# Gate rows of a hybrid mixer layer: a stage of their own, or computed beside the mLSTM projection

## The reference, cut to what matters

```python
h = _rms(x, p['norm1_g']) * (1 + sc1) + sh1
(mq, mk, mv, mi, mf, mo, gqkv, ga, gb, gz, aq, ak, av, gates) = _split(h @ p['w_in'], IN_SPLITS)
# mLSTM gates, 4 heads, 2 directions
log_i = mi.reshape(B, T, 2, M_HEADS).astype(F32) + ig_b.astype(F32)
log_f = jax.nn.log_sigmoid(mf.reshape(B, T, 2, M_HEADS).astype(F32) + fg_b.astype(F32))
# delta rule gates
g = -jnp.exp(A_log.astype(F32)) * jax.nn.softplus(ga.reshape(B, T, 2, G_HEADS).astype(F32) + dt_bias.astype(F32))
beta = jax.nn.sigmoid(gb.reshape(B, T, 2, G_HEADS).astype(F32))
```

## Time and profile before

| | us |
|---|---|
| median of three timed runs | 6535.48 |
| profiled execution, its own time | 6504.0 |
| span of the profiled execution, first to last instruction | 6502.2 |
| first norm of layer 1, 99 to 130 us, PE busy | 9.84 of 31.00 |
| gate rows of layer 1, 130 to 176.5 us, PE busy | 24.32 of 46.50 |
| projection of the mLSTM, 189 to 305 us, PE busy | 115.96 of 116.00 |

### The profile page before, as it was taken

How to read it: one execution, slowest core, us unless ns; L and a number is a source line. 1 busy time by engine, 2 the same in 40 slices (tenths; PEclk the granted TensorE clock), 3 DMA queues, 4 the chain that set the end, 5 groups by cost and what they waited for, 6 DMA issues and landing times. The chain is left out here.

```text
span 6502.2 us, 69823 instructions
## 1 busy us (share of the span) xinstructions
PE 5261.9 (81%) x25140; PEld 3598.9 (55%) x25140; DVE 3462.5 (53%) x7471; ACT 1476.1 (23%) x3146; POOL 3234.1 (50%) x3088
## 2 busy tenths in 40 slices
PE   5878877995888888888768788679958888888877
PEld 4866767894444444443248768679944444444432
DVE  6154534226666666666361644341266666666663
ACT  4222123111222222222142221231112222222221
POOL 1222321124777777777612223211247777777775
PEclk8978988997999999999979889889979999999999
DMA  5110000216999999999852100102179999999998
GB/s 200 56 45 7 1 14 26 91 59 231 409 406 405 404 402 405 405 405 396 345 184 59 41 7 1 34 11 88 59 254 409 406 405 405 403 404 404 405 389 346
DMA packets 521162, 1531.89 MB, mean 236 GB/s; under 512 B 56478, under 2 KB 154718, under 8 KB 520552
## 3 DMA queue, kind: packets, MB, share of 16 engines
q0 software_dynamic: 369024, 1342.47, 52.5%
q1 hardware_dynamic: 149708, 184.85, 8.7%
q10 hardware_dynamic: 2080, 0.01, 0.0%
HBM read 1522.06 MB, written 5.09 MB: 235 GB/s over the span
## 5 line engine op out<-in xcount | busy, mean ns | idle before, releaser
L1897 PE MATMUL pb<-vb,x_diags 128*128 128x512 f32 x5120 | 2495.9, 611 | 611.9 <-DMA vb<-in_p_v,x_idx 597.2
L1758 DVE CUSTOM_DVE_ANT_0 ub<-ub,h 128x1024 f32<-128x1024 f32 x1280 | 1567.4, 1225 | 1061.3 <-DMA ub<-in_p_u,x_idx 1051.2
L1897 PEld LDWEIGHTS pb<-vb,x_diags 128*128 128x128 f32 x5120 | 873.1, 189 | 1513.3 <-issue 1268.5
L1697 POOL DMA_INDIRECT ub<-in_p_u,x_idx x1280 | 1293.7, 1011 | 500.9 <-issue 363.5
L1697 POOL DMA_INDIRECT vb<-in_p_v,x_idx x1280 | 1274.5, 996 | 410.7 <-issue 227.3
L1867 PEld LDWEIGHTS pb<-h2T,Wq 128*128 128x128 f32 x2560 | 459.2, 192 | 506.1 <-issue 503.7
L1837 ACT ACTIVATE x_diags<-identity,x_coefs 128x128 f32<-128x128 f32 x1280 | 416.6, 392 | 581.0 <-PE pb L1897 531.2
L1867 PE MATMUL pb<-h2T,Wq 128*128 128x128 f32 x2560 | 470.2, 275 | 1.6 <-DVE kT L1784 1.6
L250 PE MATMUL pb<-e_Whi,hS_hi 128*128 128x256 f32 x1280 | 381.6, 298 | 27.9 <-DVE e_Wlo L1595 27.8
L251 PE MATMUL pb<-e_Wlo,hS_hi 128*128 128x256 f32 x1280 | 359.5, 281 | 0.0
L252 PE MATMUL pb<-e_Whi,hS_lo 128*128 128x256 f32 x1280 | 359.0, 280 | 0.0
(11 more groups left out here) (383 smaller groups left out, 8453.6 us busy)
## 6 DMA issues: line engine op xcount, KB each, us to landing
adaW<-in_ada_w SPq DMA_DIRECT2D x24, 2048.0 KB, 9.4
e_Wg<-in_w_in SPq DMA_DIRECT2D x24, 1024.0 KB, 6.0
ub<-in_p_u,x_idx POOLq DMA_INDIRECT x1280, 6.9
vb<-in_p_v,x_idx POOLq DMA_INDIRECT x1280, 6.9
m_W<-in_w_in SPq DMA_DIRECT2D x16, 1024.0 KB, 5.6
Wq<-in_p_wq SPq DMA_DIRECT2D x8, 2048.0 KB, 16.0
g_W<-in_w_in SPq DMA_DIRECT2D x12, 1024.0 KB, 5.4
modAB<-mod_rows SPq DMA_DIRECT2D x16, 512.0 KB, 6.0
```

What stands on the lines that cost most here:

```text
L1697: G.indirect_dma_start(ring[:, n % RING, :], None, table, bass.IndirectOffsetOnAxis(ap=idx[:, i % LIVE, s:s + 1], axis=0)).then_inc(in_[n ...
L1758: V.tensor_tensor_reduce(out=ub[:, n % RING, :], in0=ub[:, n % RING, :], in1=h2[:, t, :], scale=1.0, scalar=0.0, op0=ALU.mult, op1=ALU.add ...
L1897: last = mm(pb[2 * (t % 2) + j][:, :], diag[:, n % DRING, :], vb[:, n % RING, 512 * j:512 * j + 512], start=(h == 0 and s == 0), stop=(h = ...
```

## The change

`stage_rows` is gone. `gate_rows` holds the same computation as pieces that `project` calls at certain places of its programs. The first norm no longer writes exact rows: ACT writes both halves of a tile's rounded rows from PSUM, DVE both halves of the low part, from PSUM and the rounded rows. The gate weights are split in two parts on POOL and multiplied by `product`, in the form of jobs 0 to 15. The projection uses banks 0 to 3, the gate products banks 4 to 7. The raw weight buffers go from three to two. Seven rows of a common buffer replace ten; its first four are later overwritten by the output gate. The scan of b no longer reads rows that reset it, but starts anew in each 128 tokens.

```diff
-                with ExitStack() as exact:
-                    hT = sb(exact, "hT", [P, KD, TOK])
-                    with stage():
...
-                        stage_norm(0, ahead=load_constants)
-                    with stage():
-                        stage_rows(l)
+                    stage_norm(0, ahead=load_constants, split=hS)
...
+                            if split:
+                                for j in range(2):
+                                    act.wait_ge(s_tr, 2 * t + j + 1)
+                                    S.activation(split[0][:, 4 * j:4 * j + 4, t * P:(t + 1) * P], v4(pb[2 * (t % 2) + j][:, :]), ACT.Copy).then_inc(s_evA, 1)
...
+                            if t >= 1 and split:
+                                for j in range(2):
+                                    dve.wait_ge(s_evA, 2 * t - 1 + j)
+                                    part = (slice(None), slice(4 * j, 4 * j + 4), slice((t - 1) * P, t * P))
+                                    V.tensor_tensor(split[1][part], v4(pb[2 * ((t - 1) % 2) + j][:, :]), split[0][part], ALU.subtract).then_inc(s_evV, 1)
...
+        def gate_rows(l, scope, rowbuf):
...
+            Z, e_, LF, LI, SG, m_, b = [rowbuf[:, j, :] for j in range(7)]
+            AI, WK, EM = Z, e_, LF
...
+            def gpsimd_after(pool, n):
+                if n != 0:
+                    return
...
+                link(G.tensor_copy(w16s[0][:, :, :, :], w16[:, :, :, :]))
+                link(G.tensor_tensor(w16s[1][:, :, :, :], w16[:, :, :, :], w16s[0][:, :, :, :], ALU.subtract))
...
+            def tensor_at(pe, i):
+                if i == 4:
+                    pe.wait_ge(r_wc, 16)
+                    for j, (w, done) in enumerate(((w1, r_p1), (w2, r_p2))):
+                        for k2, (o, n) in enumerate(HALVES):
+                            product(pb[4 + 2 * j + k2][:, 0:n], lambda a, k: w[a][:, k, :], lambda a, k: hS[a][:, k, o:o + n], KD).then_inc(done, 1)
+                elif i == 16:
+                    pe.wait_ge(r_dsel, 1)
+                    mm(pb[4][:, 0:80], ones, dsel[:, :, :].rearrange("p c r -> p (c r)"), start=True, stop=True).then_inc(r_dec, 1)
...
+                if 16 <= i < 16 + NT:
+                    t = i - 16
...
+                    for j, a in enumerate((AI, WK, EM, SG)):
+                        last = tr(pb[5 + t % 2][:, j * P:(j + 1) * P], a[:, t * P:(t + 1) * P], ident)
...
+            def scalar(act, i):
+                if i == 0:
+                    act.wait_ge(r_small, 16 * 10)
+                    S.activation(sc2[:, 1:2], small[:, 2:3], ACT.Exp).then_inc(r_ea, 1)
+                elif i == 4:
+                    act.wait_ge(r_absz, 1)
+                    S.activation(e_, e_, ACT.Exp, scale=-1.0).then_inc(r_exp, 1)
...
+                elif i == 11:
+                    act.wait_ge(r_ai0, 1)
+                    S.activation(AI, AI, ACT.Exp).then_inc(r_ai, 1)
...
+                for c in range(NT):
+                    f, g = slice(c * P, (c + 1) * P), slice((c + 1) * P - 1, c * P - 1 if c else None, -1)
+                    scan(out=b[0:64, f], data0=ones[0:64, :], data1=LF[0:64, f], initial=0.0, op0=ALU.mult, op1=ALU.add)
+                    last = scan(out=b[64:P, g], data0=ones[64:P, :], data1=LF[64:P, g], initial=0.0, op0=ALU.mult, op1=ALU.add)
...
+                            if n == 0 and "sync_first" in beside:
+                                beside["sync_first"](sp)
...
+                            if "tensor_at" in beside:
+                                beside["tensor_at"](pe, i)
...
-                    project("mproj", chunks, jobs)(l, *weight_buffers(wst, "m"))
+                    beside = gate_rows(l, wst, rowbuf)
+                    project("mproj", chunks, jobs, beside, nb=4)(l, *weight_buffers(wst, "m", 2))
```

More of the change, by code:

```diff
@@ L326, in _, with stage_norm @@
                                                    in1=gains[:, j, :], op0=ALU.add, op1=ALU.mult).then_inc(mod_done, 1)
-        def stage_norm(which, h_keep=None, ahead=None):
+        def stage_norm(which, h_keep=None, ahead=None, split=None):
             s_in, s_sq, s_ms, s_rt, s_rs, s_mul, s_h, s_tr, s_evA, s_evV = [
@@ L383, in _ @@
                             pe.wait_ge(s_h, t + 1)
-                            if t >= 2:
+                            if t >= 2 and split:
+                                pe.wait_ge(s_evV, 2 * (t - 1))
+                            elif t >= 2:
                                 pe.wait_ge(s_evA, t - 1)
@@ new lines, in gate_rows, with sync @@
+            mp = sb(scope, "mp", [P, 3, NT])
+            dsel = sb(scope, "dsel", [P, NT, 16])
+            seg = lambda a: a.rearrange("p (c s) -> p c s", c=NT)
+            def sync(sp):
+                for j, o in enumerate((O_MI, O_GA)):
+                    sp.dma_start(w16[:, j, :, :], dram_cols(A["w_in"], l, o, 16)).then_inc(r_w, 16)
+                sp.wait_ge(r_clr, 1)
+                for q in range(4):
+                    d, isg = q // 2, q % 2
+                    column = lambda a: a[l, d, :].rearrange("(h o) -> h o", o=1)
+                    r = slice(32 * q, 32 * q + 4)
+                    if isg:
+                        sp.dma_start(small[r, 0:1], column(A["g_dt_bias"])).then_inc(r_small, 16)
+                        sp.dma_start(small[r, 2:3], column(A["g_A_log"])).then_inc(r_small, 16)
+                    else:
+                        sp.dma_start(small[r, 0:1], column(A["m_fg_b"])).then_inc(r_small, 16)
+                        sp.dma_start(small[r, 1:2], column(A["m_ig_b"])).then_inc(r_small, 16)
+                        sp.dma_start(small[r, 3:4], column(A["state_mlstm_m"][0])).then_inc(r_small, 16)
@@ L548, in program @@
+            return dict(sync_first=sync, sync_after=sync_after, gpsimd=gpsimd, gpsimd_after=gpsimd_after, tensor_at=tensor_at, scalar=scalar, vector=vector)
         CW = 256
@@ L554, in program, with project @@
         HALVES = ((0, 320), (320, 320))
-        def project(name, chunks, jobs, beside=None):
+        def project(name, chunks, jobs, beside=None, nb=8):
             beside = beside or {}
```

281 lines of the change are left out of this document (119 added, 162 removed).

## The result

The changed kernel takes 6474.0 us (median of 7 runs, 6457.9 to 6500.8) against 6529.0 for the kernel before (7 runs beside them, 6524.5 to 6542.2): a ratio of 0.993, with a 95% interval of 0.991 to 0.995, so 55 us less. Run again later, it took 6478.6 against 6521.9, 0.9936 (0.9915 to 0.9957), 43 us less. The forecast was 49 less; 6474.0 lies in its range of 6468 to 6512, near the lower end.

A forecast was written before the change was run, and what follows sets the result against it. PE was taken to bound the projection, with the gate stage ahead adding its whole length. Terms -91.0 + 5.4 + 28.2 + 5.4 + 3.0 = -49.0 gave a median of 6486.5 us from 6535.5, range 6468 to 6512.

The forecast's parts named there:

- The stage goes: Gate stage between norm and projection: its whole length is saved, 45.88 and 45.08 us in the two layers, -91.0 in all.
- Norm, +2.7: First norm: subtracting both halves on DVE where it copied one costs 2.7 us a layer, 5.4 in all.
- Gate products, 14.1: Projection, between jobs 3 and 4: four products of 3.52 us on PE, not hidden, 14.1 a layer, 28.2 in all.
- Transposes and decay product, 2.7: Projection, ahead of jobs 16 to 20: twenty transposes and one small product on PE, 2.7 us a layer, 5.4 in all.
- Start of the projection, 0: Projection's start: the narrow gate loads behind chunk 0 cost nothing; bound 3.0 us a layer if they hold it up.
- The chain beside the projection, 3.3 to spare: Gate chain during the projection: chunk 4 ready before PE asks, 3.3 us to spare if POOL's subtraction holds DVE's scans.
- Stage end, +1.5: mLSTM stage's end: clearing 60 semaphores where there were 35 costs 1.5 us a layer, 3.0 in all.
- A's stand: Projection at job 16: the chain comes late, PE stands and restarts slowly, 8.5 us a layer, 6503.5; chance 0.12.
- B's dear norm: First norm: every copy and subtraction of a tile stands in line, 10.5 us in all, 6502; chance 0.07.
- C's 13.24: Projection: chain not hidden, PE's present 13.24 us wait comes back, 21.7 a layer with 8.5 more, 6530; chance 0.05.
- D: Projection after a new wait: clock falls to 0.50 for the rest, at most 57 us a layer more, 6600; chance 0.03.

The follow-up runs named there:

- own stage: The changed kernel with all gate work again in a stage of its own between norm and projection; 6531.3 us, 1.0018 to the kernel before.
- the norm with chunk 0: The changed kernel with the projection's chunk 0 loaded, rounded and subtracted while the norm runs; 6457.6 us, 0.9897 to the kernel before.
- the kernel with the chain 10 late: The changed kernel with 12 more DVE operations (10.2 us) inside the gate chain; 6477.5 us (one run).
- filled scan: The changed kernel with six unused 128x128 PE products ahead of each mLSTM scan round's second update; 6446.4 us, 0.9892 to the kernel before.

## Why the prediction was right, point by point

The forecast for the stretch was -45.9 + 2.7 + 14.1 + 2.7 = -26.4 in layer 1; measured -25.9. In layer 2 it was -25.6, measured -25.7. By its steps:

- **The stage goes**: right. Alone, the moving is worth 27.3 and 25.8 a layer (own stage against the changed kernel, 204.2 - 176.9 and 202.8 - 177.0). The projection's first load stands 2.1 behind the norm's last DVE work, as forecast.
- **Norm, +2.7**: right. DVE's last work ends at 131.53 where it ended at 128.84, +2.69; a tile takes 3.65 where it took 3.05. DVE of the changed kernel:

```profile
118.32 1.27 DVE L370 SCALAR_TENSOR_TENSOR h<-x,nrm_ss,modAB 128x1024 f32<-128x1024 f32 x1
...
121.97 1.27 DVE L370 SCALAR_TENSOR_TENSOR h<-x,nrm_ss,modAB 128x1024 f32<-128x1024 f32 x1
...
130.84 0.69 DVE L378 TENSOR_TENSOR hS_lo<-pb,hS_hi 128x512 fp32r<-128x512 f32 x1 [0.16 <-ACT hS_hi L354]
```

- **Gate products, 14.1**: right. ACT's evacuations of jobs 3 and 4 lie 17.61 apart, one job of 3.52 and 14.09:

```profile
162.83 0.44 ACT L647 ACTIVATE m_qT<-pb 128x320 f32<-128x320 f32 x1 [3.08 <-PE pb L245]
...
180.44 0.44 ACT L647 ACTIVATE m_qT<-pb 128x320 f32<-128x320 f32 x1 [15.37 <-PE pb L245]
```

- **Transposes and decay product, 2.7**: near, 2.4. The copies of the columns come every 3.32, and jobs of 256 columns without transposes come every 2.88 later in the same trace, so 0.44 a tile and 2.2 for five, beside the decay product's 0.2. Those jobs came every 2.85 before; the 0.03 is 0.6 over twenty jobs, which the forecast had at nothing and no run explains.
- **Start of the projection, 0**: off by 1.0 in the dear direction (13.04 us from the first load to the first product, 12.05 before), inside its bound of 3.0. All of it is chunk 0's landing, 6.50 from its issue to ACT's rounding where it was 5.50; with the narrow loads behind it it is 5.7 to 6.6 in six profiles, and 5.5 in the own stage, where chunk 1 follows it. The first job gave 0.8 of it back (5.6 to its evacuation for 6.3), so the two nearly cancel. ACT and PE of the changed kernel:

```profile
140.15 1.91 ACT L637 ACTIVATE m_Whi<-m_W 128x2048 fp32r<-128x2048 f32 x1 [9.34 <-DMA m_W<-in_w_in]
...
146.69 0.63 PE L243 MATMUL pb<-hS_hi,m_Whi 128*128 128x320 f32 x1 [16.51 <-POOL m_Wlo L609]
```

- **The chain beside the projection, 3.3 to spare**: right, with the hold that no row had shown. The third scan, a form that takes 0.41, took 4.66 beside POOL's subtraction of chunk 3, so the AI rows ended at 207.76, 45.0 behind the products' start (forecast 44.9), and chunk 4 was ready at 216.39, 53.6 behind it (53.8). PE reached the decay product at 218.95 and job 16 at 219.49, so 3.1 were spare. DVE, POOL and PE:

```profile
194.26 4.66 DVE L530 TENSOR_TENSOR_SCAN m_rows<-m_rows 32x128 f32<-32x128 f32 x1
...
206.93 0.83 DVE L546 TENSOR_TENSOR m_rows<-alpha,mp 128x640 f32<-128x640 f32 x1
...
193.32 5.33 POOL L609 TENSOR_TENSOR m_Wlo<-m_W,m_Whi 128x2048 fp32r<-128x2048 f32 x1 [23.55 <-ACT m_Whi L637]
...
211.78 4.61 POOL L609 TENSOR_TENSOR m_Wlo<-m_W,m_Whi 128x2048 fp32r<-128x2048 f32 x1 [13.13 <-ACT m_Whi L637]
...
218.95 0.34 PE L468 MATMUL pb<-dsel,con 128*128 128x80 f32 x2
...
219.49 0.37 PE L243 MATMUL pb<-m_Whi,hS_hi 128*128 128x256 f32 x1
```

The Trainium skill, SBUF — State Buffer, Who interferes with whom, was weighed here: a VectorE instruction with two SBUF inputs and a GpSimd instruction that reads SBUF exclude each other for the whole instruction. The trace agrees for a scan (4.66 for 0.41), and the norm with chunk 0 for a scalar-tensor-tensor (3.96 for 1.27).
- **Stage end, +1.5**: a little small. From the gain's load to the next stage's first load it takes 21.0 and 20.4 where it took 18.8 and 18.6, +2.2 and +1.8, inside the bounds of 1.2 to 2.3. It goes with the semaphores and not with the scan: 20.4 to 22.3 in the nine profiles with 60 of them, 18.6 to 18.8 in the two with 35. The next stage's first load in layer 1, before and changed (the gain's load stands at the end of the scans above):

```profile
421.76 0.31 SPq L1151 DMA_DIRECT2D g_cwr<-in_g_conv_w  x1
```
```profile
403.05 0.31 SPq L1176 DMA_DIRECT2D g_cwr<-in_g_conv_w  x1
```

- **Rivals**: A's stand and B's dear norm didn't come; C's 13.24 is hidden (the own stage shows 15.79 for it); D was seen in small in the kernel with the chain 10 late, and its price was one slow job. One slip in the forecast's sums had no weight: D is said to decide for slower from 24.5 a layer, but that only brings the time back to before's; its own bound of 6548.6 takes 31.
- **What the sum left out**: the scan. The terms that were there came to -47.6 (-25.9 - 25.7 + 2.2 + 1.8), against -49.0. The clock in the scan then moves a layer by up to 14 us either way (90.8 to 104.8 in unfilled scans), and layer 2's expert stage, whose code is the same in all, took 1756.1 us in before's profile and 1770.4 in the changed kernel's (second norm's load to the first store of the output), and 1747.9 to 1770.4 over the eleven profiles. The scans' 10.0 and these 14.4 bring the 47.6 to 23 for the profiled pair, whose spans differ by 19.6; the other 3.6 lie between the stage end and the second norm, 1.4 in layer 1 and 2.2 in layer 2, and stay unexplained. I'd ascribe the distance from 47.6 to the medians' 55 and 43 to the same two, which isn't shown; no run separates them in the timed executions. That the medians came out this near to 49 is partly luck, since the scans alone can move one execution by more than half of it.

What stays open: why the clock falls in one execution's scan at a given round and not in another's, why it fell in the filled scan of layer 2, and whether it falls as often in the kernel before as in the changed one.

## What to carry to other kernels

A stage whose engine waits for a chain is worth its whole length when it can stand beside one that keeps that engine busy; what it costs there is only the busy engine's own instructions, counted one by one, and whether the chain fits is a sum over the waits in front of it. Before a change is blamed for a longer stretch behind it, look at the granted clock there and profile the same program again. Where PE waits a microsecond or two in every round of a dense loop, put the next round's independent products there: here that took another 40 us off (6457.6 to 6417.2; by the ratios to before 37, with some 27 either way), of the same order as the change under study.

## What the runs showed of the hardware that was not expected

- The granted clock fell to 0.50 in a loop where PE waited at most 2.1 us at a time, and stayed there for 15 us while PE was busy throughout (298 to 313). The mLSTM scan of one program took 90.85 and 104.79 us in one execution.
- A DVE scan, and an operation on two SBUF tiles, were held to about the end of a POOL subtraction that was under way: 4.66 us for 0.41, 3.96 for 1.27.
- SP took 2.60 us to issue two narrow loads right behind the load of chunk 0 (1.85 to 2.74 in layer 1 of the six profiles of that order), and 1.02 where they stood first.
